# Context rows of two experts scattered in one rounded TensorE pass

## The reference

```
def _expert_choice_ffn(h, w_router, w1, w3, w2):
    B, T, D = h.shape
    cap = CAPACITY_FACTOR * T // N_EXPERTS
    aff = jax.nn.softmax((h @ w_router).astype(jnp.float32), axis=-1)
    vals, idx = lax.top_k(aff.transpose(0, 2, 1), cap)
    xg = jax.vmap(lambda hb, ib: hb[ib])(h, idx)
    hid = jax.nn.silu(jnp.einsum('becd,edf->becf', xg, w1)) * jnp.einsum('becd,edf->becf', xg, w3)
    y = jnp.einsum('becf,efd->becd', hid, w2) * vals[..., None].astype(h.dtype)
    return jax.vmap(lambda yb, ib: jnp.zeros((T, D), h.dtype).at[ib.reshape(-1)].add(yb.reshape(-1, D)))(y, idx)
```

## Time and profile before

| | us |
|---|---|
| median of 3 runs | 3771.17 |
| lowest and highest | 3766.63, 3771.34 |
| the profiled execution | 3768.74 |
| its span (first to last instruction) | 3766.7 |
| first layer's expert loop (PE) | 1407.9 to 2046 |
| second layer's expert loop (PE) | 3122 to 3722 |

### The profile page before, as it was taken

How to read it: one execution, slowest core, us unless ns; L and a number is a source line. 1 busy time by engine, 2 the same in 40 slices (tenths; PEclk the granted TensorE clock), 3 DMA queues, 4 the chain that set the end, 5 groups by cost and what they waited for, 6 DMA issues and landing times.

```text
span 3766.7 us, 49816 instructions
## 1 busy us (share of the span) xinstructions
PE 3401.9 (90%) x19108; PEld 2788.2 (74%) x19108; DVE 2276.4 (60%) x3357; ACT 1621.1 (43%) x2095; POOL 615.1 (16%) x480
## 2 busy tenths in 40 slices
PE   7998899899999969999997399998999969999994
PEld 4997678888887857777775288678766657788873
DVE  3696741511111649999997684742332257999997
ACT  3114742411110237777774322753211127777762
POOL 2001012212121012221211200112222101111110
PEclk9999999999999979999998599998999979999997
DMA  7332133022222329999997122121123217999994
GB/s 248 101 137 94 46 102 124 13 73 73 74 90 78 104 89 336 328 326 334 335 338 258 58 90 79 51 91 46 52 89 101 85 74 280 350 344 362 357 341 173
DMA packets 331923, 632.85 MB, mean 168 GB/s; under 512 B 14526, under 2 KB 104910, under 8 KB 325358
## 3 DMA queue, kind: packets, MB, share of 16 engines
q1 hardware_dynamic: 309056, 557.88, 42.4%
q0 software_dynamic: 22704, 72.68, 5.8%
HBM read 614.00 MB, written 16.50 MB: 167 GB/s over the span
## 4 chain that ended last, share of the span: by engine, by line
PE 71%; DVE 13%; ACT 6%; issue 4%; DMA 4%; DVEq 0%; POOL 0%; ACTq 0%; SPq 0%; POOLq 0%
PE ps L851 43%; PE ps L1265 17%; DVE part L2092 2%; PE ps L981 2%; PE ps L1013 2%; ACT hx L1536 2%; DVE area L1696 1%; PE ps L999 1%; DMA raw<-in_w_exp_gate 1%; ACT area L1388 1%; PE ps L1001 1%; DMA raw<-in_w_exp_up 1%; DVE area L2100 1%; ACT area L1315 1%; DVE stat L1606 1%
## 5 line engine op out<-in xcount | busy, mean ns | idle before, releaser
L851 PE MATMUL ps<-hx,part 128*128 128x384 f32 (+2 forms) x4704 | 929.4, 356 | 11.1 <-POOL part L518 5.5
L851 PEld LDWEIGHTS ps<-hx,part 128*128 128x128 f32 x4704 | 830.3, 189 | 98.6 <-issue 23.2
L1265 PE MATMUL ps<-part,hx 128*128 128x512 f32 x3072 | 752.1, 398 | 16.6 <-ACT part L1536 11.0
L1265 PEld LDWEIGHTS ps<-part,hx 128*128 128x128 f32 x3072 | 578.3, 191 | 149.2 <-ACT part L1536 12.7
L2092 DVE TENSOR_TENSOR part<-raw,part 128x2048 fp32r<-128x2048 f32 x256 | 593.2, 2319 | 100.4 <-ACT part L1536 99.2
L1536 ACT ACTIVATE part<-raw 128x2048 fp32r<-128x2048 f32 x256 | 490.2, 1916 | 157.2 <-PE ps L1265 88.9
L1265 PE MATMUL ps<-hx 128*128 128x512 f32 x1536 | 382.6, 398 | 8.9 <-ACT hx L1536 7.2
L518 POOL TENSOR_TENSOR part<-raw,part 128x2048 fp32r<-128x2048 f32 x52 | 237.9, 4575 | 821.2 <-ACT part L515 821.2
L1265 PEld LDWEIGHTS ps<-hx 128*128 128x128 f32 x1536 | 290.0, 190 | 81.7 <-ACT hx L1536 11.0
L851 PE MATMUL ps<-part,hx 128*128 128x256 f32 (+2 forms) x2208 | 315.0, 305 | 18.3 <-DVEq L532 15.5
L2092 DVE TENSOR_TENSOR hx<-raw,hx 128x2048 fp32r<-128x2048 f32 x128 | 295.9, 2311 | 57.8 <-ACT hx L1536 56.2
(11 more groups left out here) (256 smaller groups left out, 3706.0 us busy)
## 6 DMA issues: line engine op xcount, KB each, us to landing
raw<-in_w_exp_gate SPq DMA_DIRECT2D x128, 1024.0 KB, 5.7
raw<-in_w_exp_up SPq DMA_DIRECT2D x128, 1024.0 KB, 5.9
raw<-in_w_exp_down SPq DMA_DIRECT2D x128, 1024.0 KB, 6.5
raw<-in_w_mod SPq DMA_DIRECT2D x48, 1024.0 KB, 6.0
raw<-in_w_in SPq DMA_DIRECT2D x44, 1024.0 KB, 5.5
raw<-in_w_gate SPq DMA_DIRECT2D x32, 1024.0 KB, 7.9
area<-in_bias POOLq DMA_DIRECT2D x32, 512.0 KB, 4.0
raw<-in_w_branch SPq DMA_DIRECT2D x16, 1024.0 KB, 7.2
```

Of the source, the lines that this page charges most:

```text
L851: last = mm(dst, a, b, start=i == 0, stop=i == len(pairs) - 1)
L1265: last = mm(ps[:, bank, :], x, y, start=kh == 0 and a == 0, stop=kh == 1 and a == len(pairs) - 1)
```

## The change

In the first layer an expert's 32 context rows are put twice among the operand columns, so that PE delivers them twice, on two groups of 32 partitions. ACT writes the rounded high part to both groups. DVE then overwrites the second group with the low part. `y_ctx` and `put_ctx` now lie in `hx` (fp32r), and `put_ctx` has its ones on both groups. One rounded 128x512 pass over all 128 partitions then adds high and low parts of both experts of a pair. `slot_c` is `slot_col` with the second group's numbers lowered by 32, so that both groups compare with the same slots.

```
@@ -432,14 +432,16 @@
-        y_ctx, o = cut(work, o, D)
-        put_ctx, o = cut(work, o, CTX)
...
-        rows_of = [(slice(0, CAPL), slice(CAPL, CAP)), (slice(P - CAPL, P), slice(0, CAPC))]
+        rows_of = [(slice(0, CAPL), slice(CAPL, P)), (slice(CAPL, P), slice(0, CAPL))]
+        high_of = [slice(CAPL, CAPL + CAPC), slice(0, CAPC)]
+        low_of = [slice(CAPL + CAPC, P), slice(CAPC, CAPL)]
...
+        y_ctx, o = cut(hx, o, D)
+        put_ctx, o = cut(hx, o, CTX)
@@ -776,7 +779,8 @@
-                        moves = [(rows_of[j][0], src[:, :, 0:CAPL]), (rows_of[j][1], src[:, :, CAPL:CAP])][:2 if full == NT else 1]
+                        moves = [(rows_of[j][0], src[:, :, 0:CAPL]), (high_of[j], src[:, :, CAPL:CAP]),
+                                 (low_of[j], src[:, :, CAPL:CAP])][:3 if full == NT else 1]
@@ -790,7 +794,7 @@
-                                     slot_d[l, v, bass.ds(e, 1), LAT:TOK].to_broadcast([CAPC, CTX])
+                                     slot_d[l, v, bass.ds(e, 1), LAT:TOK].to_broadcast([2 * CAPC, CTX])
@@ -1268,7 +1272,7 @@
-                                scatter(c, 4, slice(0, P) if c < 2 * TL else slice(0, CAP))
+                                scatter(c, 4, slice(0, P))
@@ -1276,7 +1280,7 @@
-                    scatter(c, c % 4, slice(0, P) if c < 2 * TL else slice(0, CAPC))
+                    scatter(c, c % 4, slice(0, P) if c < 2 * TL else rows_of[1][1])
@@ -2115,14 +2119,14 @@
-                            for (a, z, r), dst in zip(sets, (put, put_ctx)):
-                                last = V.tensor_scalar(dst[r, :], pair[r, 0, a:z], slot_col[r, :], None, ALU.is_equal)
+                            for (a, z, r), dst, col in zip(sets, (put, put_ctx), (slot_col, slot_c)):
+                                last = V.tensor_scalar(dst[r, :], pair[r, 0, a:z], col[r, :], None, ALU.is_equal)
@@ -2135,9 +2139,11 @@
-                            r = rows_of[j][0]
-                            V.scalar_tensor_tensor(y_lo[r, c], ps[r, 5 + half, :], val[r, 0:1], y_hi[r, c].bitcast(f32),
-                                                   ALU.mult, ALU.subtract).then_inc(*S("e_yL", l).by(1))
+                            lows = [(rows_of[j][0], y_lo, y_hi), (low_of[j], y_ctx, y_ctx)][:2 if ctx_out else 1]
+                            for r, dst, rounded in lows:
+                                last = V.scalar_tensor_tensor(dst[r, c], ps[r, 5 + half, :], val[r, 0:1],
+                                                              rounded[r, c].bitcast(f32), ALU.mult, ALU.subtract)
+                            last.then_inc(*S("e_yL", l).by(1))
@@ -2145,6 +2151,10 @@
+                own(V.tensor_copy(slot_c[:, :], slot_col))
+                own.wait()
+                for r in low_of:
+                    own(V.tensor_scalar(slot_c[r, :], slot_col[r, :], -float(CAPC), None, ALU.add))
```

More of the change, by code:

```diff
@@ L452, in build @@
         stat = sb("stat", [P, 2, 18])
+        slot_c = sb("slot_c", [P, 1])
         stage = S("stage_done")
@@ L2117, in turn @@
                             dve.wait_ge(*S("pair_in", l).at(i * 32 * nload + 16 * nload * (j + 1)))
-                            for a, z, r in sets:
-                                last = V.scalar_tensor_tensor(vscr[r, a:z], pair[r, 0, a:z], slot_col[r, :], pair[r, 1, a:z],
+                            for (a, z, r), col in zip(sets, (slot_col, slot_c)):
+                                last = V.scalar_tensor_tensor(vscr[r, a:z], pair[r, 0, a:z], col[r, :], pair[r, 1, a:z],
                                                               ALU.is_equal, ALU.mult, accum_out=val[r, 0:1])
```

## The result

The changed kernel is slower by 0.6%: 3794.66 us median of six runs (3785.62 to 3800.26) against 3770.39 for the kernel before, measured beside it; the ratio is 1.0058 with a 95% interval of 1.0046 to 1.0071. The forecast was 3773 with a range up to 3785, so both miss. The profiled execution has a span of 3791.6 us, 24.9 above that of before.

The account below looks back on a forecast made before the run. PE was the busier engine over a pair, but its second half was DVE's list with only 2.69 us spare. Terms 0.7 + 0.7 + 1.8 + 0.3 + 0.7 - 1.0 = +3.2 us gave 3773 us, range 3762 to 3785.

Parts of the forecast that it names:

- the sum on DVE: Second expert's block 2 to the next pair's: DVE arrives 0.1 us later per pair, +0.7 over seven passages.
- gaps of 2.69 us: DVE's three gaps between second expert's block 2 and next pair's, 0.69, 0.93 and 1.07, to be used up.
- Turn 1 was counted at 1.4: At the first expert's end, two new DVE operations make its next low part start 1.4 us later.
- PE was taken to set the pace of the first expert and DVE that of the second: Within a pair: first half stays PE's; PE's 2.5 us saving lies in the second half, where DVE has 2.69 spare.
- POOL: One more copy and subtraction per expert, 1.5 us, hidden except for L2119: 0.1 per pair, +0.7, bounds 0 and 0.4.
- 0.3 ahead of the loop: Ahead of the expert loop, three one-column DVE operations per layer: +0.3 us in all.
- The clock: PE waits about 2.5 us more per pair, so one more fall of its granted clock: +1.8 us.
- the ends: Ahead of the loop +0.3; behind the last pair +0.7 before the last scatters, then -1.0 for four context scatters.
- PE's saving is worth nothing: Second expert: scatters save PE 2.5 us per pair, but it waits that long for DVE's low parts.
- The size of DVE's new operation: Low part of the context rows, 32 partitions by 512 columns: 0.70 us each, 2.8 per pair.
- PE sets the pair: Rival: DVE's delay is caught up, PE keeps 1.0 us per pair, -7, so 3764; chance 0.20.
- The weight stream becomes the bound: Rival: later slot release and earlier block requests cost 1 us per pair in loads, +7, 3780; chance 0.11.

Follow-up runs that it names:

- E12: Kernel before plus the two new DVE low-part operations per expert, writing to spare columns of hx; scatters float32, no second POOL group: 3787.63 us, ratio 1.0033.
- P: PE's one-pass rounded context scatter in place of the float32 one; with only this part of the change kept, 3773.62 us, ratio 1.0001.
- E3: Changed kernel without DVE's new low-part operations and POOL's second copy and subtraction, so only the single rounded scatter stays: 3773.62 us, ratio 1.0001.
- E4: Kernel before with POOL copying and subtracting the 32 context columns a second time into spare rows: 3778.34 us, ratio 1.0017.
- E9: Kernel before with only half of each expert weight block loaded in layer one, all engine work kept: 3763.22 us, ratio 0.9971.
- E10: Single rounded scatter alone (low part of context rows left out), with half of each expert block loaded in layer one: 3757.73 us, ratio 0.9953.
- D: The two new DVE low-part operations per expert; added alone to the kernel before, writing to spare columns: 3787.63 us, ratio 1.0033.
- E11: Whole changed kernel with only half of each expert weight block loaded in layer one: 3782.88 us, ratio 1.0028.
- E2: Changed kernel without POOL's copy and subtraction for the second group of context columns: 3784.80 us, ratio 1.0025.
- G: POOL's second copy and subtraction of the context columns; added alone to the kernel before, into spare rows: 3778.34 us, ratio 1.0017.
- E6: Changed kernel with the router values computed at b = 5 instead of b = 9: 3798.91 us, ratio 1.0068.
- E7: Changed kernel, new DVE operations at b = 2, 3 of the next expert, context scatters at b = 5 to 8, router values at b = 5, hidden product first: 3804.91 us.
- E1: Changed kernel without DVE's new low-part operations, the low part of the context rows not computed: 3779.31 us, ratio 1.0016.

## Why the prediction was wrong

**The step that failed** is the sum on DVE: "1533.72 + 35.71 + 1.4 = 1570.83 ... Net: 0.1 us later per pair, if every gap is used up". The new operations were to vanish into gaps of 2.69 us. Alone on the kernel before they cost 2.1 a pair (E12), with P and POOL's part 2.6. Three things were off.

- DVE's work was taken as fixed, 35.71 us, wherever it stands. The gaps did fill for the most part: in the pair shown 0.73 of 2.69 are left, and the 1.07 ahead of block 2, directly behind the new operations, is gone. But in body 2 the work itself grew. Low parts that start inside POOL's copies and subtractions take up to 3.06 for 2.29 in the changed kernel, 0.65 a pair in the mean, so body 2 shrank by 0.4 for 1.6. This meeting comes from the shift in time, as E12 and E3 show, where POOL does no more than before.
- Turn 1 was counted at 1.4 and its gain left to body 2. It has no gap of its own but 0.33, ahead of the new work. Two operations with their spacing make 1.7 there, not 1.4 (E12).
- PE was taken to set the pace of the first expert and DVE that of the second. Body 1 is 28.5 in every kernel of the table whatever PE saved or DVE was given. But the turns at both ends are DVE's, and PE waits there at two new places each (0.71 and 0.42; 0.81 and 0.44), and 1.71 in the body between.

**POOL** is the second mis-sized term: 0.1 a pair in the sum, with a bound of 0.4; measured 0.9 (E4), of which 0.49 is one router-value operation behind a subtraction. The row that showed it once stood in turn 2 of the first pair; that one more copy and subtraction, put at 1.5 us, would push POOL's work into turn 1 of each pair was not worked out. POOL ended 2.1 us ahead of L2119, and the additions come to 2.7 (2.27 to 2.61 for the copies, 3.94 to 6.34 for the subtractions, before against E4). The rest of its price, 0.4 to 0.5, is in turn 2, where L2121 of that kernel meets POOL again, 1.12 for 0.75. At the head of the stage PE now waits 1.25 for POOL's subtraction (L789), where the prediction put down 0.3 ahead of the loop, for DVE; that stretch is 2.8 longer, 2.7 of it in E4 as well.

**The clock** is the third mis-sized term: one more fall, +1.8, was counted, and the profiled execution has two fewer, -3.5. Of **the ends**, the last scatters' wait for DVE is 3.02 for 2.26, +0.8 where 0.7 was put down, as foreseen.

**PE's saving is worth nothing**: right, and shown by E3 (+0.8 us). The reason given was half of it. That the second expert is DVE's list holds in its turns. In its body the saving is lost to waits for ACT and to low parts that POOL's work lengthens, and both go with half the loads, where P is worth 1.3 a pair (E9, E10).

**The size of DVE's new operation** was right: 0.75 for the 0.70 taken, 0.75 on 32 and on 64 partitions alike.

**The rivals.** "PE sets the pair" needed half the loads, and even then had no chance against D: E11 is 79.7. "The clock falls in every pair" fell outright: the changed kernel has 1.00 in all seven pairs, before 0.98 in two; falls come with P instead (0.98 in all but one pair of E3, in every second one of E10). The Trainium skill, page "TensorE: Matmul & The Clock Gate", section "A second HAM failure mode: psum-queue depth-cycling", lets frequent short waits bring the clock down; here kernels with many such waits (after, 5.8 us in six a pair; E11, 5.5 in six; E12, 3.2 in five) hold 1.00 throughout, and E3 and before, with fewer of 0.4 us or more, two and one, lose it at times. E2 has after's waits less POOL's share and 0.96 in three pairs. So the count of short waits doesn't decide it here, against that rule; what does is open. "The weight stream becomes the bound": the sign that the prediction named did come. ACT's waits for loads in the seven pairs (1420 to 1980) grew from 39.8 to 53.4 us, 1.9 a pair where 0.5 was the limit. Yet with half the loads, where these waits are nearly gone, a pair is still 79.7 (E11), so they have little share in the loss; in the missing gain they have one.

**What stays open.** D alone costs 12.3 us, G alone 5.5, P alone 0.8, together 18.6 of the 24.3 measured. The 95% intervals of these differences are 3 to 5 us to either side each, so the other 5.7 may be chance. In the single traces it is the other way round: from the first to the last expert matmul of layer one, D adds 15.1 us, G 7.8 and P 4.9, and the whole change 20.5. In the pairs, D's 2.1 and G's 0.9 make 3.0 for 2.6. No run settles more than that. That it is POOL's use of something which DVE's low parts share that lengthens them is inferred from the order of starts in the timelines; no run takes POOL's copies away from that place. Nor was it followed up when POOL's work and DVE's low parts meet: it shifts with PE's pace and the loads. No version was found that beats the kernel before with its full loads: moving work along DVE's list (E6, E7) only moved the loss.

## What to carry to other kernels

When work is put on an engine that runs a list in order, cut the loop at records of that list, and put each new operation in its own segment with the gaps of that segment alone: here the turn that got the new work had 0.33 of gap and paid in full. Gaps further on did fill in part, but the later start brought the operations there beside another engine's work, and half of what was won went into longer operations. So read the lengths of the old operations again as well as the gaps. Before work is moved from an engine at 75 of 77 us to one at 73 of 77, add it up on the receiving engine first: DVE's busy time grew by 4.5 us a pair to take 2.5 off PE, and the loop paid 2.6. Work on POOL that nobody waits for is not free where operations of DVE then start before POOL has ended.

## What was not expected of the hardware

A 64x512 operation of DVE with two operands in SBUF took 1.14 us on average when POOL had one more subtraction in flight near it (E1, E4), for 0.79 in the kernel before and 0.74 in E2. A 128x2048 low part took 3.06 for 2.28 when it started 0.36 us after POOL's series of subtractions had begun, and 2.28 when it started just ahead of one. The added subtraction lengthened POOL's own series by 2.4 where one had measured 1.11. DVE's cost did not depend on partitions (0.751 us on 32, 0.750 on 64, E12). PE's granted clock was 1.00 in all seven windows of a kernel that waits 5.8 us a pair in six pieces, and 0.98 in every second pair of one that waits less (E10), at 1.6 us a fall.
